# Sample tokens' dilated attention in four 32-column groups of the array, unrolled, with the first keys and values fetched beside the last retention head

## The reference

```
A_PATTERNS = ((128, 1), (512, 4), (2048, 16))
def dilated_window_decode(q, k_all, v_all, slopes, window, dil):
    offs = jnp.arange(window // dil + 1) * dil
    idx = nbuf + jnp.arange(T)[:, None] - offs[None, :]
    kg = jnp.take(k_all, idx, axis=1)
    vg = jnp.take(v_all, idx, axis=1)
    s = jnp.einsum('bthe,btkhe->bhtk', q, kg) * (Dh ** -0.5) - slopes[:, None, None] * offs
    lse = jax.nn.logsumexp(s, axis=-1)
    p = jnp.exp(s - lse[..., None])
    o = jnp.einsum('bhtk,btkhe->bthe', p, vg)
parts = [dilated_window_decode(qa, k_all, v_all, slopes, w, d) for (w, d) in A_PATTERNS]
o_a = combine_patterns(parts)      # softmax over the three lse
```

## Time and profile before

| what | us |
|---|---|
| median of 3 runs | 3420.89 |
| the profiled execution's own time | 3423.01 |
| its span, first to last instruction | 3421.3 |
| PE busy | 3128.2 (91%) |
| mean granted TensorE clock | 0.958 of full |

### The profile page before, as it was taken

One profiled execution on the slowest core, in us unless ns is written; L12 is line 12 of the kernel. 1 busy time (PEld: TensorE's weight loads), 2 busy tenths in 40 slices (PEclk: granted clock), 3 DMA queues, 4 the chain that ended last, 5 costly groups with the idle time before them and its releaser, 6 DMA issues. The chain is left out here.

```text
span 3421.3 us, 50617 instructions
## 1 busy us (share of the span) xinstructions
PE 3128.2 (91%) x20146; PEld 2773.2 (81%) x20146; DVE 1417.3 (41%) x2751; ACT 847.9 (25%) x1588; POOL 321.5 (9%) x313
## 2 busy tenths in 40 slices
PE   2999999698999999999888999978889999999997
PEld 2888899445999999999855666655688999999997
DVE  4244444333454444444422222233335544444445
ACT  3344312112222211211212223222323221121113
POOL 3111132110300000000100000022213000000001
PEclk6999999898999999999999999989989999999998
DMA  3221111551188921110001000045411211111101
GB/s 121 79 63 45 51 45 45 211 172 59 50 295 290 318 77 37 61 49 25 7 34 45 15 8 15 8 155 186 156 56 56 62 49 37 37 61 49 37 25 54
DMA packets 207706, 277.45 MB, mean 81 GB/s; under 512 B 16027, under 2 KB 179477, under 8 KB 202133
## 3 DMA queue, kind: packets, MB, share of 16 engines
q1 hardware_dynamic: 195032, 152.04, 14.4%
q0 software_dynamic: 12544, 123.61, 10.2%
HBM read 258.47 MB, written 84.07 MB: 100 GB/s over the span
## 5 line engine op out<-in xcount | busy, mean ns | idle before, releaser
L784 PE MATMUL psum<-mlp_halves,w_up 128*128 128x352 f32 x6336 | 1021.0, 323 | 17.1 <-DVE mlp_halves L514 13.7
L784 PEld LDWEIGHTS psum<-mlp_halves,w_up 128*128 128x128 f32 x6336 | 1016.0, 189 | 19.7 <-DVE mlp_halves L514 14.8
L822 PE MATMUL psum<-acts,w_down 128*128 128x352 f32 x3168 | 514.9, 323 | 7.8 <-DVE xT L965 6.4
L822 PEld LDWEIGHTS psum<-acts,w_down 128*128 128x128 f32 x3168 | 508.9, 188 | 10.4 <-DVE xT L965 7.6
L1407 PE MATMUL psum<-h_ab,w_in_halves 128*128 128x352 f32 x2016 | 341.9, 327 | 38.1 <-POOL w_in_halves L1707 37.1
L965 DVE TENSOR_TENSOR xT<-xT,psum 128x352 f32<-128x352 f32 x528 | 274.5, 520 | 237.1 <-PE psum L822 237.1
L1407 PEld LDWEIGHTS psum<-h_ab,w_in_halves 128*128 128x128 f32 x2016 | 323.2, 189 | 52.4 <-POOL w_in_halves L1707 37.6
L871 ACT CAST acts<-window 128x1056 fp32r<-128x1056 f32 x44 | 47.4, 1077 | 706.7 <-PE psum L822 572.3
L461 POOL TENSOR_TENSOR norm_temps<-norm_temps 128x352 f32<-128x352 f32 x72 | 76.4, 1073 | 1447.4 <-ACT norm_temps L452 1444.6
L585 PE MATMUL psum<-mlp_halves,project_w 128*128 128x352 f32 x1152 | 189.8, 328 | 15.1 <-DVE project_w L613 15.1
L585 PEld LDWEIGHTS psum<-mlp_halves,project_w 128*128 128x128 f32 x1152 | 188.5, 192 | 15.8 <-DVE project_w L613 15.3
(11 more groups left out here) (323 smaller groups left out, 3576.9 us busy)
## 6 DMA issues: line engine op xcount, KB each, us to landing
mlp_raw<-in_w_up SPq DMA_DIRECT2D x88, 512.0 KB, 5.1
out_new_a_k_s<-in_cache_a_k POOLq DMA_DIRECT2D x8, 4088.0 KB, 15.5
out_new_a_v_s<-in_cache_a_v POOLq DMA_DIRECT2D x8, 4088.0 KB, 15.2
mlp_raw<-in_w_down SPq DMA_DIRECT2D x22, 1024.0 KB, 6.2
w_in_raw<-in_w_in_ab SPq DMA_DIRECT2D x28, 512.0 KB, 4.6
ws_k_rows<-in_cache_a_k SPq DMA_DIRECT2D x8, 1024.0 KB, 8.0
ws_v_rows<-in_cache_a_v POOLq DMA_DIRECT2D x8, 1024.0 KB, 8.2
ws_k_rows<-in_cache_a_k SPq DMA_DIRECT2D x24, 256.0 KB, 3.5
```

The costliest lines, as they stand in the source:

```text
L784: mm = nc.tensor.matmul(c.bank[TILES * part + n][:, 0:TILE], w_up[s][:, w, part, k, :], h[:, x, k, tokens_of(n)], start=k + w + x == 0, st ...
L822: mm = nc.tensor.matmul(c.bank[6 + t % 2][:, 0:TILE], w_down[:, w, s, o * P:(o + 1) * P], acts[s][:, x, tokens_of(n)], start=s + w + x == ...
```

## The change

**Column groups.** The four chunks h no longer add up in one accumulation. Chunk h writes its scores to partitions 32h to 32h+31, of which 8 rows (its two heads times 4 tokens) are used; tables, mask and pick table are laid out for 128 partitions. `weigh` likewise takes for each chunk only its own 128 value columns. Scores of a sample are one tile of 928 columns over two banks, and one fused VectorE instruction adds the bias, negates and takes the minimum.

**Order and rings.** All steps are unrolled. Key transposes go through three banks; `ws_kT` has two buffers; values have three buffers; the query tile is filled once for all samples.

**Transfers.** `first_keys` (5 tables, keys of samples 0 and 1) is issued by SP and `first_values` (values of samples 0 and 1) by POOL, in the mixer, once all projections are done. The restore of `xT` moves behind the last keys, and two blocks of `w_out` are fetched ahead of it (`project.early`).

```
+        if hd == B_HEADS - 1:
+            sp.wait_ge(projected, START + TILES * CHUNKS)
+            samples.first_keys(sp)
         sp.wait_ge(state_ready, START + QB * (hd + 1))
         sp.dma_start(d["new_ret_p"][0, 0, hd], state[:, QB, :]).then_inc(ret_stored, 16)
...
+    pool.wait_ge(projected, START + TILES * CHUNKS)
+    samples.first_values(pool)
...
-    def sync(self, sp):
-        for o in range(KC):
+    def sync(self, sp, begun):
+        for o in range(2 if begun else 0, KC):
...
+    K_RING, V_RING = 2, 3
+    def first_keys(self, sp):
+        for dst, name in ((self.bias[0][:, 0:self.PAST], "past_bias"), (self.bias[1][:, 0:self.PAST], "past_bias"),
+                          (self.new_bias[:], "new_bias"), (self.own_head[:], "own_head"), (self.pick[:], "pick_step")):
+            sp.dma_start(dst, d[name]).then_inc(self.tables_in, 16)
+        for b in range(self.K_RING):
+            self.load(sp, "k", b)
...
+            def _(sp):
+                for b in range(self.K_RING, DEC_BATCH):
+                    sp.wait_ge(k_turned, START + key_unit(b - self.K_RING, G - 1) + 1)
+                    self.load(sp, "k", b)
+                project.early(sp, w_out)
                 sp.dma_start(c.xT[:], c.spill).then_inc(c.restored, 16)
...
+            def _(pool):
                 nc.gpsimd.memset(queries[:], 0.0).then_inc(q_cleared, 1)
+                self.load(pool, "v", 2)
+                ...
+                for b in range(DEC_BATCH):
+                    if b + self.V_RING < DEC_BATCH:
+                        pool.wait_ge(valued, START + b + 1)
+                        self.load(pool, "v", b + self.V_RING)
...
-                    for h in range(HC):
-                        keys = k_sample[:, h, :] if lo == PAST else kT[:, h, lo:hi]
-                        mm = nc.tensor.matmul(c.bank[bank][0:32, 0:hi - lo], queries[:, h, :], keys, start=h == 0, stop=h == HC - 1)
+                    for lo, hi in ((0, 512), (512, PAST)):
+                        for h in range(HC):
+                            nc.tensor.matmul(scores[rows_of_chunk(h), lo:hi], queries[:, h, b, :], kT[b % 2][:, h, lo:hi], start=True, stop=True)
...
-                    for g in range(KG):
-                        nc.tensor.matmul(c.bank[4][0:32, :], probs_T[:, g, :], v_rows[s][:, g, :], start=g == 0, stop=False)
+                    for g in range(G):
+                        for h in range(HC):
+                            nc.tensor.matmul(c.bank[OUT][rows_of_chunk(h), 0:P], probs_T[:, g, rows_of_chunk(h)], v_rows[b % self.V_RING][:, g, h * P:(h + 1) * P],
+                                             start=g == 0, stop=False)
...
-                        for h in range(HC):
-                            mm = nc.tensor.matmul(c.bank[7][:, at:at + DEC_SEQ], out[:, h * P:(h + 1) * P], pick[:], start=True, stop=True)
+                    nc.tensor.matmul(c.bank[OUT][:, 256:256 + HC * DEC_SEQ], out[:], self.pick[:], start=True, stop=True).then_inc(spread, 1)
...
+                for b in range(DEC_BATCH + 2):
+                    if b < DEC_BATCH:
+                        turn_keys(b, range(0, 3))
+                    if b >= 2:
+                        spread_out(b - 2)
+                    if b < DEC_BATCH:
+                        turn_keys(b, range(3, G))
+                    if 1 <= b <= DEC_BATCH:
+                        turn_probs(b - 1)
+                    if b < DEC_BATCH:
+                        score(b)
+                    if 1 <= b <= DEC_BATCH:
+                        weigh(b - 1)
...
-                        nc.vector.reduce_max(row_max[:], scores[:], AX_X).then_inc(max_found, 1)
+                        nc.vector.tensor_tensor_reduce(probs[:], scores[:, 0:KEYS], bias[b % 2][:], -1.0, 3e38, ALU.add, ALU.min,
+                                                       neg_max[:, b:b + 1]).then_inc(biased, 1)
```

372 lines of the change are left out of this document (185 added, 187 removed).

## The result

The changed kernel takes 3323.57 us, the median of 4 runs (3316.14 to 3330.75), beside 3421.47 us for the kernel before on the same chip (4 runs, 3420.22 to 3426.11): a ratio of 0.9711, 95% interval 0.9688 to 0.9735. Forecast were 3319 us and a range of 3303 to 3341. The profiled execution took 3316.14 us, its span 3314.3. One thing was not forecast: the changed kernel's runs lie 15 us apart, where those of before lie 6 apart.

The account below looks back on a forecast made before the run. TensorE bounds the samples' stage, and once its step shrinks the transfers do. Stage -100.1 us, projection -2.6, added barrier +1: -101.7 us against the median 3420.9 gives 3319 us, range 3303 to 3341.

Parts of the forecast that it names:

- TensorE's step: One sample's work on TensorE in the samples' attention stage: 8.5 us against 19.61.
- The changes of the array's shape: Switching TensorE between transposes and 32-column products: 0.2 us each for three a step, 0.6 us in all.
- rival 4: Slower than before: four array-shape changes a step, 32 in all, drain TensorE; at 5 us each 3468 us; chance 0.01.
- 66 forecast: First to sample 7's transposes: 20.2 MB of loads at 0.343 take 58.9 us, plus about 7 half used: 66 us.
- 7 us that are half used: Early in the samples' stage, until both load queues are filled, about 7 us of transfer time are only half used.
- The tail: Last sample's work in the stage, from its key transposes to the last copy, covered by nothing: 14.2 us.
- 6 for the store: The sample states' store, behind the early loads on SP's queue, makes the barrier before the stage 6 us late.
- SP's queue alone: From 604 to 610.5, before the values' loads, SP's queue at about 0.3 moves 1.9 of its 5.4 MB.
- The early fetch: First keys and values loaded in the mixer: the stage's own 16.0 us wait goes, minus 6 for a late barrier.
- Column groups in turn: Rival 3: the four column groups take turns on TensorE, step 18.5 us, stage 70 us longer, 3389 us; chance 0.03.
- Rival 1: TensorE's chain binds the stage, not the transfers, which run at 390 or more: 3308 us; chance 0.20.
- Rival 2: Slower transfers in the stage, 300, or keys under half beside values: 3329 us, 3337 with a lower clock; chance 0.20.

Follow-up runs that it names:

- a0_after: The changed kernel again, no edit, 4 runs beside three experiment kernels: 3313.75 us, ratio 0.9693 to the kernel before.
- f1_after: The changed kernel a third time, no edit, 5 runs on another chip, profile of its slowest run: 3323.50 us, ratio 0.9716 to the kernel before.

## Why the prediction was right, and where it was not

The total came out inside the range and 4.6 us from the forecast: 97.9 us less in the medians against 101.7. The mechanism is the forecast one: TensorE's step falls to 8 us, then the keys' transfers bind, and the start is late by the store. Within it errors cancel, and some luck is in the number (2).

1. **TensorE's step.** Forecast 8.5 us, measured 8.05: transposes of keys with the spread 3.50 (3.55 forecast), of probabilities 0.96 (0.98), scores 1.59 (1.65), values 2.00 (1.76). The changes of the array's shape, 0.6 in the sum, leave no gap between the rows: that term was too large, and the row it came from the earlier trace rows bounded it at 0.1 each, 0.3 in all. (The sum counted three changes a step, rival 4 four.) That the overlap of the groups makes the gain of the values is shown by the groups in turn, which take back 26.8 of those 38.2 us; for the scores it rests on the rows alone. VectorE and ScalarE have 5.97 and 5.18 us busy in a full window of 10 us, that is 4.8 and 4.2 a step (4.8 and 4.1 forecast). TensorE waits for their copies of keys 2.6 us in all, with the first two samples (9.1 us before, in all steps): the PSUM copies did not become the bound that the Trainium skill, "TensorEngine Tiling (Array Packing)", section "Performance Considerations", warns of.
2. **Then the transfers bind.** Right in kind: the waits are named by the keys' DMA and go with the bytes (fewer bytes, xT's fetch first). The form was not as forecast: not steps of 10 to 11 us from the fourth on, but steps of 8.05 with two waits, and a second step of 9.7 (648.83 - 639.13) where 8.5 stood. And yet sample 7's transposes began 66.7 us after the first (66 forecast). Three terms of that 66 were off. The rate in full windows is 372 to 387 GB/s, not 343: that makes 53 us of the 59 for 20.2 MB. The windows above move some 22.5 MB by then, 2.3 more than counted, most of sample 7's values among them: 6 us. And the lull of the DMA engines, two windows at 0.58 and 0.77, lost 6.5 us. The prediction speaks of 7 us that are half used, which would lose 3.5 and give 62.4; its sum added the whole 7. So the near hit is the higher rate against bytes left out, with a slip in the sum that came close to the real lull. The other profiles, 64.1 us (a0_after) and 71.6 (f1_after), show how far that number moves by itself. The tail was 14.2 us, as forecast. The Trainium skill, "DMA: Bandwidth & Descriptors", section "Where 436 GB/s comes from", has about 358 on the HBM side of one core, half of what two cores share; the full windows here, with one core running, stand above it.
3. **The start of the stage.** SP's last wait 10.4 us (8 to 12 forecast), first transposes at 631.49 (631 to 636, though with a mixer that ended 2.0 us early), 8.9 us behind VectorE's end where a change of stage was 2.7: 6.2 us, and 6 for the store and 1 for the barrier were forecast. With the store first the 8.9 are 4.2, so the store is 4.7 of it and the rest, the added barrier with it, 1.5. No row gave the 0.3 that the sum took for SP's queue alone.
4. **The early fetch** was priced at 10 us net (16.0 less 6); taken away it costs 18. The 16.0 came from a stage that began with fewer loads in flight; with the loads of the changed kernel the same stretch, from the stage's first instruction to the first transposes, is 24.8 us, and 24.8 less some 6 is near the 18. The forecast total does not depend on this, since it counted from the first transposes.
5. **The projection.** 3.0 us off (2.6 forecast); 3.9 by the experiment, and without it TensorE also waits 2.3 us for the last values. xT's fetch holds up nothing where it stands, as said; put first it costs 10 to 13 us.
6. **The rivals.** Column groups in turn and the change of the array's shape fall with the first profile. Rival 1 (3308) had the rate about right, yet waits remain; its time without waits is near that of the runs with fewer bytes or a third key buffer. Rival 2 (3329, 3337 with a lower clock) had the waits and the clock, which f1_after's profile shows, but not their cause: full windows there move 373 to 390 GB/s, not 300, and what is missing is in the lull (DMA shares of 0.36, 0.85 and 0.89 from 630 to 660). Nor does the clock follow the length of a wait as rival 2 had it (below). So the 13 runs of this kernel, from 3311.2 to 3330.8 us, reach from close to rival 1's number to rival 2's, without being either. That this kernel would scatter over such a range is what the forecast lacked. The ends of its range do not follow from its own terms: a store that is not late takes rival 1 to 3305, not 3303, and rival 2 with the lower clock stood at 3337, not 3341.

## What to carry to other kernels

Products that use a quarter of the array's columns can be packed fourfold, and the order of the instructions decides how far they overlap: let neighbours use different column groups, with at most some four records of one group in a row. When such a gain uncovers the transfers, look for windows with a DMA share well below 1 just after the start, since an idle moment there can be paid back as a wait (and a lower clock) later; filling it won 7.7 us in one sitting and nothing sure in another. A load that is moved ahead of a store on one queue delays the store and the barrier behind it: put the store first.

## What the runs showed of the hardware

- TensorE overlaps records of different column groups across a short run of records of one group: 30.6 ns a record (128 columns) with two of a group in a row, 31.8 with four (1.78 us for 56), 61 with eight and six (3.43), 90 with fourteen. One group at a time, 128 columns took 116 ns in the kernel before.
- A change between full-width transposes and products on 32 columns shows no gap: 678.88 to 686.93 and on without idle time.
- Keys and values together moved at 384 to 390 GB/s at DMA shares of 1.03 to 1.05, against 342 and 344 in the earlier trace rows. The two windows of before held tables too; what makes the difference no run shows.
- A store of 0.5 MB took 10.0 to 11.0 us behind 4.8 MB of loads on its own queue, with values loading on another; 2.4 to 2.7 with 1.84 MB less ahead of it, 2.6 with none.
- Behind some waits of TensorE the next twelve transposes took up to 2.82 us in place of 1.53, at a granted clock of 0.50 where they took 2.82; behind others they did not, and the length of the wait does not decide it. Slowed: waits of 1.9, of 2.4 to 2.65, of 3.7 to 4.0 and of 4.8 to 8.0 us. Not slowed: 2.7 and 3.2 us, and all up to 1.0. Two slowed rows, from the first and the second profile of the store first (the row of the third key buffer above, with 2.71 us of wait and 1.53 of transposes, is one that was not slowed):

```profile
674.94 2.82 PE L2069 MATMUL psum<-ident_sb,ws_k_rows 128*128 128x128 f32 x12 [1.92 <-DMA ws_k_rows<-in_cache_a_k]
```
```profile
695.75 2.82 PE L2069 MATMUL psum<-ident_sb,ws_k_rows 128*128 128x128 f32 x12 [2.65 <-DMA ws_k_rows<-in_cache_a_k]
```
